# A transformer block on one core: the second MLP product computed with seven block products in place of eight

## The reference

```
h  = rms_norm(x);  proj = h @ w_in                    # 512 tokens, D = 2048
x  = x + merged(attention branches, gates) @ w_out
h2 = rms_norm(x)
u  = relu(h2 @ w_mlp_up)                              # 2048 -> 8192
x  = x + (u * u) @ w_mlp_down                         # 8192 -> 2048
```

## Time and profile before

| | |
|---|---|
| median of 3 runs | 2702.49 us (2702.45 to 2702.6) |
| the profiled execution | 2704.16 us, span 2702.4 us |
| PE, PEld, DVE, ACT, POOL busy | 2693.1, 2396.2, 1712.9, 1179.5, 41.1 us |
| granted PE clock | 1.0 throughout |
| moved from and to HBM | 348.23 MB read, 37.75 MB written |

### The profile page before, as it was taken

One profiled execution on the slowest core, in us unless ns is written; L12 is line 12 of the kernel. 1 busy time (PEld: TensorE's weight loads), 2 busy tenths in 40 slices (PEclk: granted clock), 3 DMA queues, 4 the chain that ended last, 5 costly groups with the idle time before them and its releaser, 6 DMA issues.

```text
span 2702.4 us, 44449 instructions
## 1 busy us (share of the span) xinstructions
PE 2693.1 (100%) x15962; PEld 2396.2 (89%) x15962; DVE 1712.9 (63%) x2978; ACT 1179.5 (44%) x1628; POOL 41.1 (2%) x60
## 2 busy tenths in 40 slices
PE   9999999999999999999999999999999999999999
PEld 8999999788888888888899999999998888888887
DVE  4648887677777754434588788788764444444444
ACT  5534443545555552224354444444443333433343
POOL 0000000000000000000000000000000000000000
PEclk9999999999999999999999999999999999999999
DMA  6444344332232235534343433433456565565653
GB/s 249 119 128 130 125 138 123 96 85 80 72 85 77 79 107 151 142 125 154 119 133 125 135 129 124 140 124 126 138 188 223 187 222 200 193 224 186 226 200 119
DMA packets 359572, 386.96 MB, mean 143 GB/s; under 512 B 16464, under 2 KB 274000, under 8 KB 358992
## 3 DMA queue, kind: packets, MB, share of 16 engines
q1 hardware_dynamic: 331936, 347.24, 40.6%
q10 hardware_dynamic: 27568, 38.81, 4.1%
HBM read 348.23 MB, written 37.75 MB: 143 GB/s over the span
## 4 chain that ended last, share of the span: by engine, by line
PE 98%; DVE 1%; ACT 0%; DMA 0%; issue 0%; SPq 0%; ACTq 0%; DVEq 0%
PE job L1731 7%; PE job L1734 7%; PE job L1733 7%; PE job L2044 2%; PE job L2048 2%; PE job L2046 2%; PE scores L2048 2%; PE scores L2046 2%; PE scores L2044 2%; PE job L2071 2%; PE job L2073 2%; PE job L2072 2%; PE scores L2071 2%; PE scores L2072 2%; PE scores L2073 2%; PE heads_out L1831 1%
## 5 line engine op out<-in xcount | busy, mean ns | idle before, releaser
L1665 DVE TENSOR_TENSOR w_lo_d<-raw_d,w_hi_d 128x512 fp32r<-128x512 f32 x256 | 176.3, 690 | 369.0 <-ACT w_hi_d L1090 369.0
L1393 DVE TENSOR_TENSOR lo<-pair,hi 128x1792 fp32r<-128x1792 f32 x142 | 287.1, 2022 | 122.6 <-ACT hi L862 122.6
L862 ACT ACTIVATE hi<-pair 128x1792 fp32r<-128x1792 f32 x142 | 241.5, 1701 | 276.4 <-PE heads_out L2048 119.6
L1090 ACT ACTIVATE w_hi_d<-raw_d 128x512 fp32r<-128x512 f32 x256 | 161.5, 632 | 405.2 <-PE heads_out L2073 202.8
L697 ACT ACTIVATE w_hi<-raw 128x512 fp32r<-128x512 f32 x268 | 168.8, 631 | 354.7 <-PE job L1734 242.9
L1148 DVE TENSOR_TENSOR w_lo<-raw,w_hi 128x512 fp32r<-128x512 f32 x268 | 186.9, 699 | 157.5 <-ACT w_hi L697 156.4
L1731 PE MATMUL job<-a_hi,w_hi 128*128 128x512 f32 x560 | 229.5, 410 | 0.0
L1734 PE MATMUL job<-a_hi,w_lo 128*128 128x512 f32 x560 | 219.6, 392 | 0.0
L1733 PE MATMUL job<-a_lo,w_hi 128*128 128x512 f32 x560 | 218.6, 390 | 0.0
L2044 PE MATMUL job<-h,hi 128*128 128x256 f32 x512 | 145.1, 283 | 2.2 <-DVE lo L1393 2.1
L1671 DVE TENSOR_TENSOR u_lo<-u_raw,u_hi 128x2048 fp32r<-128x2048 f32 x64 | 146.2, 2284 | 0.0
(11 more groups left out here) (468 smaller groups left out, 7767.1 us busy)
## 6 DMA issues: line engine op xcount, KB each, us to landing
pair<-in_w_mlp_up SPq DMA_DIRECT2D x256, 256.0 KB, 2.9
u_raw<-u_rows SPq DMA_DIRECT2D x64, 1024.0 KB, 5.6
raw_d<-in_w_mlp_down SPq DMA_DIRECT2D x128, 512.0 KB, 6.1
raw<-in_w_in SPq DMA_DIRECT2D x79, 512.0 KB, 4.1
pair<-in_w_gate SPq DMA_DIRECT2D x84, 256.0 KB, 2.9
raw<-in_w_out SPq DMA_DIRECT2D x64, 256.0 KB, 3.3
u_rows<-u_out ACTq DMA_DIRECT2D x32, 512.0 KB, 4.3
raw<-in_w_in SPq DMA_DIRECT2D x24, 344.0 KB, 3.2
```

The costliest lines, as they stand in the source:

```text
L862: nc.scalar.activation(pair_hi[j % 2], pairs[j][:, :, 1:8], ACT.Copy).then_inc(pair_hi_ready, 1)
L1090: nc.scalar.activation(w_hi_d[:, j % SPLITS], raw_d[:, j // 2, j % 2], ACT.Copy).then_inc(down_hi, 1)
L1393: nc.vector.tensor_tensor(pair_lo[j % 2], pairs[j][:, :, 1:8], pair_hi[j % 2].bitcast(F32), ALU.subtract).then_inc(pair_lo_ready, 1)
L1665: nc.vector.tensor_tensor(w_lo_d[:, j % SPLITS], raw_d[:, j // 2, j % 2], w_hi_d[:, j % SPLITS].bitcast(F32), ALU.subtract).then_inc(down_ ...
```

## The change

The second product gets the same seven-for-eight scheme as the first. The weights `w_mlp_down` are the stationary side, in pairs of 128 output columns (`COLS` = 8 pairs of pairs, 256 columns each) and pairs of 128 rows. The 8192 rows of `u*u` are 32 slices. A *group* g takes eight of them, slices g to g+7 modulo 32, times column block g modulo 8; four groups with one column block cover all 32 slices, and there are 32 groups of four units. From one group to the next one slice leaves and one comes in, so 39 slices are loaded in all (`load_slice`, 7 combinations x 256 columns = 896 KB).

- At the end of the first product VectorE forms the combinations of `u*u` (`sum_u`, three operations of 512, 256 and 256 columns) and ScalarE stores 896 KB in place of 512 KB for each pair (`store_u`). In the loop body the store of the even pair stands ahead of the round of unit 0, that of the odd pair behind the round of unit 4.
- `sum_pairs` forms the sums of two units in one go (1024, 512 and 512 columns) at even units, in place of `sum_pair` at each. This holds for the first product too.
- In each group one new slice is rounded (ScalarE, 1792 columns) and split (VectorE, 1792 columns) at unit 3.
- The combined results of groups 0 to 7 are stored by POOL in HBM (`sum_rows`, 512 KB a group); groups 8 to 23 are added to them by accumulating DMAs, each of which waits for the one before. For groups 24 to 31 the sum is loaded, added by VectorE (`total`), turned back to tokens by eight transposes on PE (`turn_out`, ahead of unit 3 of the next group), scaled by ScalarE (`scale_out`, four operations of 256 columns) and added by an accumulating DMA to `out`, in which the residual was stored earlier (no `x2_rows` and no load of it).

```diff
-    x2_rows = nc.dram_tensor("x2_rows", (S, D), F32, kind="Internal").ap()
+    u_rows = nc.dram_tensor("u_rows", (PAIRS, P, 7 * 2 * P), F32, kind="Internal").ap()
+    sum_rows = nc.dram_tensor("sum_rows", (COLS, P, 4 * 2 * P), F32, kind="Internal").ap()
     v_rows = nc.dram_tensor("v_rows", (S, WD + WF), F32, kind="Internal").ap()
...
+            def load_down(g, j):
+
+                sp.wait_ge(pair_lo_ready, down_unit(g, j) - 3)
+                at, cols_of = (g + 2 * j) % PAIRS, slice(2 * P * (g % COLS), 2 * P * (g % COLS + 1))
+                for h in range(2):
+                    into = pairs[j][:, :, 2 * h:2 * h + 2].rearrange("p k i c -> p k (i c)")
+                    if crosses_end(g, j):
+                        sp.dma_start(into[:, 0], wd[h, :, at, cols_of]).then_inc(pair_loaded[j], 16)
+                        sp.dma_start(into[:, 1], wd[h, :, 0, cols_of]).then_inc(pair_loaded[j], 16)
                     else:
+                        sp.dma_start(into, wd[h, :, at:at + 2, cols_of]).then_inc(pair_loaded[j], 16)
+
+            def load_slice(e):
+
+                sp.wait_ge(pair_used, UPS - 3 + e // 2 if e < 8 else down_unit(e - 8, 0) + 1)
+                sp.wait_ge(u_stored, 16 * (e % PAIRS + 1))
+                sp.dma_start(h_slices[e % 8][:, :, 1].bitcast(F32),
+                             u_rows[e % PAIRS].rearrange("p (a s) -> p a s", a=7)).then_inc(slice_loaded[e % 8], 16)
+
+            for g in range(GROUPS):
+                for j in range(4):
+                    load_down(g, j)
+                    if g == 0 and j > 1:
+                        load_slice(2 * j - 4)
+                        load_slice(2 * j - 3)
+                    if g == 1 and j == 0:
+                        for e in range(4, 8):
+                            load_slice(e)
+                    if g > 0 and j == 1 and g + 7 < EVENTS:
+                        load_slice(g + 7)
...
+            def store_part(g):
+
+                pool.wait_ge(c_ready, GATE_PAIRS + PAIRS + g + 1)
+                into = sum_rows[g % COLS].rearrange("p (a s) -> p a s", a=4)
+                if g < COLS:
+                    pool.dma_start(into, blocks[:, 0:4]).then_inc(part_stored, 16)
+                else:
+                    pool.wait_ge(part_stored, 16 * g)
+                    pool.dma_start(into, blocks[:, 0:4], accum_op=ALU.add).then_inc(part_stored, 16)
+
+            def load_sum(g):
...
+            def add_out(g):
+
+                pool.wait_ge(out_scaled, g - CLOSING + 1)
+                q = g % COLS
+                pool.dma_start(outt[:, :, 2 * P * q:2 * P * (q + 1)], out_tok[:, :, :], accum_op=ALU.add
+                               ).then_inc(out_added, 16)
...
+            def store_u(p):
+
+                act.wait_ge(u_summed, p + 1)
+                into = u_rows[p] if isinstance(p, int) else u_rows[bass.ds(p, 1)].rearrange("a p c -> p (a c)")
+                act.dma_start(into, u_blocks[:, 1:8].rearrange("p a s -> p (a s)")).then_inc(u_stored, 16)
...
+                    if m == 0 and not first:
+                        store_u(i * 2 - 2)
...
@@ -1075,62 +1102,62 @@
                     if not (first and m < 4):
                         round_pair(n, m % 4, n - 1)
                     if m == 2 and not first:
-                        finish_pair(i * 2 - 1, 1)
+                        finish_pair(i * 2 - 1)
+                    if m == 4 and not first:
+                        store_u(i * 2 - 1)
                     if m == 6:
-                        finish_pair(i * 2, 0)
+                        finish_pair(i * 2)
 
...
+            def scale_out(g):
+
+                act.wait_ge(out_turned, g - CLOSING + 1)
+                at_least(act, out_added, 16 * (g - CLOSING))
                 for b in range(TB):
+                    last = nc.scalar.activation(out_tok[:, b], bank_sets[g % 2][b // 2][:, 2 * P * (b % 2):2 * P * (b % 2 + 1)],
+                                                ACT.Copy, scale=r2[:, b:b + 1])
+                last.then_inc(out_scaled, 1)
...
+            def sum_pairs(n, j):
...
+                nc.vector.tensor_tensor(t[:, :, 4:6], t[:, :, 1:3], t[:, :, 0:1].broadcast_to([P, 4, 2, P]),
+                                        ALU.add).then_inc(sums_first, 2)
+                dve.wait_ge(sums_first, n + 2)
+                nc.vector.tensor_tensor(t[:, :, 6], t[:, :, 4], t[:, :, 2], ALU.add).then_inc(sums_second, 2)
+                dve.wait_ge(sums_second, n + 2)
+                nc.vector.tensor_tensor(t[:, :, 7], t[:, :, 6], t[:, :, 3], ALU.add).then_inc(sums_ready, 2)
+
...
+            def total(g):
+
+                dve.wait_ge(sum_loaded, 16 * (g - CLOSING + 1))
+                dve.wait_ge(c_fourth, GP + PAIRS + g + 1)
+                dve.wait_ge(c_ready, GP + PAIRS + g + 1)
+                nc.vector.tensor_tensor(sum_in[:, 0:4:2], blocks[:, 0:4:2], sum_in[:, 0:4:2], ALU.add)
+                nc.vector.scalar_tensor_tensor(sum_in[:, 1:4:2], blocks[:, 1:4:2], -1.0, sum_in[:, 1:4:2], ALU.mult,
+                                               ALU.subtract).then_inc(total_ready, 1)
...
+                p = GP + PAIRS + g - 1
+                for j in range(4):
+                    n = down_unit(g, j)
                     if j == 1:
+                        combine_early(p, (g - 1) % 2, blocks)
+                    split_pair(n, j)
+                    if j == 1:
+                        combine_late(p, (g - 1) % 2, blocks)
+                        if g > CLOSING:
+                            total(g - 1)
+                    if g == 0 and j < 3:
+                        split_slice(2 * j + 2)
+                        split_slice(2 * j + 3)
+                    if j % 2 == 0 and n + 2 < down_unit(GROUPS, 0):
+                        sum_pairs(n + 2, (j + 2) % 4)
+                    if j == 3:
+                        if g == 0:
+                            sum_u(PAIRS - 1)
+                        if g + 8 < EVENTS:
+                            split_slice(g + 8)
...
+            def turn_out(g):
+
+                pe.wait_ge(total_ready, g - CLOSING + 1)
+                for b in range(TB):
+                    for i in range(2):
+                        at = 2 * P * (b % 2) + P * i
+                        last = nc.tensor.transpose(bank_sets[g % 2][b // 2][:, at:at + P],
+                                                   sum_in[:, 2 * (b // 2) + 1 - i, P * (b % 2):P * (b % 2 + 1)],
+                                                   ident[:, :])
+                last.then_inc(out_turned, 1)
+
+            for g in range(GROUPS):
+                pe.wait_ge(c_ready, GATE_PAIRS + PAIRS + g - 1)
+                at_least(pe, out_scaled, g - 1 - CLOSING)
+                for j in range(4):
+                    if g > CLOSING and j == 3:
+                        turn_out(g - 1)
+                    pe.wait_ge(slice_ready, g + 2 * j + 2)
+                    up_unit(down_unit(g, j), j, g % 2, at=g)
+            turn_out(GROUPS - 1)
```

More of the change, by code:

```diff
@@ L619, in _ @@
-            sp.wait_ge(pair_used, UPS - 3)
-            for c in range(BLOCKS):
-                down_loads(c, 0)
-                down_loads(c, 1)
-                load_back(c)
-                with sp.Fori(2, KD // (2 * KU)) as turn:
-                    down_loads(c, turn)
+            wd = w_mlp_down[0].rearrange("(s h p) c -> h p s c", h=2, p=P)
+            def load_down(g, j):
[6 more added lines that the diff above has]
+                        sp.dma_start(into[:, 1], wd[h, :, 0, cols_of]).then_inc(pair_loaded[j], 16)
+                    else:
+                        sp.dma_start(into, wd[h, :, at:at + 2, cols_of]).then_inc(pair_loaded[j], 16)
@@ L1120, in _, with round_slice @@
-            round_u(0, 0, 0)
-            for n in range(LEAD):
-                if n == 2:
-                    copy_p1(GP + PAIRS - 1, 1, blocks)
-                round_down(n, n)
-            finish_pair(PAIRS - 1, 1)
-            for c in range(BLOCKS):
-                down_turn(c, 0)
-                with act.Fori(1, KD // (2 * KU) - 1) as turn:
-                    down_turn(c, turn)
-                down_turn(c, KD // (2 * KU) - 1)
-            store_out(BLOCKS - 1)
-            for b in range(TB):
-                act.wait_ge(out_stored[b], 16 * BLOCKS)
+            def round_slice(e):
+                act.wait_ge(slice_loaded[e % 8], 16 * (e // 8 + 1))
+                slot = h_slices[e % 8]
+                nc.scalar.activation(slot[:, :, 0], slot[:, :, 1].bitcast(F32), ACT.Copy).then_inc(slice_hi, 1)
@@ L1136, in _ @@
+            act.wait_ge(total_ready, GROUPS - 1 - CLOSING)
+            copy_p1(GP + PAIRS + GROUPS - 1, (GROUPS - 1) % 2, blocks)
+            scale_out(GROUPS - 1)
         @block.vector
@@ L1621, in _ @@
             split_pair(GU + 1, 1)
[L1622 to L1623 removed]
+            sum_pairs(GU + 2, 2)
             combine_acts(6)
@@ L1647, in up_pairs @@
                         combine_late(i * 2 + GP, 0, blocks)
```

(25 more changed lines are left out.)

301 lines of the change are left out of this document (116 added, 185 removed).

## The result

| | before | after |
|---|---|---|
| median | 2702.55 us (2702.45 to 2702.65) | 2806.99 us (2803.63 to 2811.93) |
| ratio of the runs | | 1.0388, interval 1.037 to 1.0406 |
| span of the profiled run | 2702.4 us | 2801.9 us |

3.9% slower, where 1.3% was forecast. The page after, parts 1, 4 and 5, against the earlier trace rows: PE has gaps now, and the chain, 98% PE before, is 56% PE.

The account below looks back on a forecast made before the run. PE was taken to bound the kernel, the second product by its pace alone. Terms -52.4 + 6.1 + 31 + 10.7 + 17.3 + 7.8 + 10.5 + 5 = +36 gave 2738 us; range 2692 to 2795.

Parts of the forecast that it names:

- Accumulating DMAs elsewhere: Groups 8 to 23 of the second product: adding transfers mostly hidden, sharing DMA engines with slices and weights; +5 us, bounds 0 and 50.
- The prediction's own sign of being wrong: The forecast is wrong if the first product takes 650 us, or the second's groups 20.2 or above 22 us.
- The passage: From unit 0 to unit 1, both products: two units' sums make PE 0.50 us late, 62 times, +31 us.
- The store: First product's loop: even pair's store ahead of unit 0's round makes it 0.71 us late, 15 times, +10.7 us.
- PE's own work: Second product: 128 units of 5.04 us take 645.1 us for 697.5, -52.4 us; transposes add 6.1 us.
- The opening: Start of the second product: eight slices must land, be rounded and split; PE waits, +17.3 us, bounds 8 and 30.
- The tail: After the last matmul: 14 us for 3.5, with 7 us for the accumulating DMA; +10.5 us.
- Passage hidden: Rival at unit 0 to unit 1: two units' sums cost no more than one's; 2685 us, chance 0.17.
- Weights late: Rival in the second product: each group waits for weights at unit 2's sums; 2769 or 2805 us, chance 0.19.
- Slow accumulate: Rival: from 20 us on the accumulating DMA paces groups 8 to 23; 2810 to over 2900 us, chance 0.07.

Follow-up runs that it names:

- single sums: The changed kernel with one unit's block sums at every unit in both products, in place of two units' sums at every second: 2764.88 us, ratio 1.0222.
- the last kernel: The changed kernel with single sums, even-pair store behind the round, slice rounded at unit 1, split at unit 2, opening slices loaded earlier, `scale_out` later: 2687.52 us.

## Why the prediction was wrong

**The failed step is "Accumulating DMAs elsewhere", with what it left out.** It took +5 us for all traffic in the loop, and looked for a consumer of late transfers at the sums of unit 2. The consumer was the slice's round and split at unit 3, in the opening priced with care and in the loop not at all. Moving these two took 31.1 us off groups 8 to 23, loading a seventh of the slice 31.5, plain stores 18.2. So the term was late slices, 31 us, of which 18 went when the transfers beside them didn't add in memory. The prediction's own sign of being wrong, groups above 22 us, came true in groups 8 to 30 (23.05 and 23.15 on average).

**The passage: mechanism right, size too small.** 0.50 forecast; with the store out of the way a group of the first product is 0.68 to 0.74 over: 0.50, 0.14 from the handovers, and up to 0.10 at unit 2. In groups 8 to 23 single sums saved 15.8 us, where 16 x 0.50 = 8 was forecast. They also ended VectorE's waits for late weights there (none between 2220 and 2500 us, 30.1 us in the change), since a sum over two units waits for the weights of both. How much of the 15.8 that is was not taken apart.

**The store: right, 0.71 forecast, 0.95 measured** (14.2 / 15). From the start of the round of unit 3, `sum_u` ends at +5.29 in a passage of the loop (1515.72 to 1521.01), where +5.27 was forecast. From there to the round lie 0.69 us (0.17 to the issue of the store, 0.52 from the issue to the round), where 0.48 was forecast: these two handovers were taken too short.

**PE's own work: right.** Units are 5.04 us wherever nothing is late, in two kernels through 23 groups. A unit behind eight transposes is 5.86: 0.82, for 0.87 forecast.

**The opening: nearly right, 20.3 for 17.3.** Its five gaps were forecast at 4.4, 7.9, 1.1, 3.4 and 0.5 us and measured 5.7, 8.5, 2.2, 2.4 and 1.6, so that one error partly covers the others. The clock had no place in the estimate. PE issued 53 matmuls in 8 us at a mean granted clock of 0.73 (2058 to 2066), 151 ns each for 120. In the whole opening 59 matmuls were issued at 0.50, each some 0.09 us longer than at full clock: an estimate of at most 5.5 us, since waits behind them hide a part.

**The tail: 17.4 us for 14.** The work ahead of the transfer took 7.6 us (2784.47 to 2792.06), where its terms add to 6.6. From the last scaled piece (2790.49 + 1.57) to the end of the span are 9.8 us, 1.3 of them POOL's issue; 7 had been taken for the transfer, from bounds and without a row:

```profile
2792.36 1.30 POOL L688 DMA_DIRECT2D out<-out_tok  x1 [9.71 <-ACT out_tok L1126]
```

**The rivals.** "Passage hidden" fell: single sums save 42 us. "Weights late" had the time nearly right and the place wrong: its 2805 us for 3 us a group, near the measured 2807, is luck. The waits are there, up to 4.1 us, but with the slices out of the way they cost little. "Slow accumulate" fell in its form, since no part waits 20 us, and was right in spirit: the addition costs what stands beside it.

The sign of the prediction held, and mostly for the reasons given: the passage, the store, the opening and the tail came as forecast or larger. The size failed because each engine's fixed order was checked at one place, the passage from unit 0 to unit 1, and not where the change itself had added new waits.

What stays open: why 128 KB of a slice need 7.7 us to land, and how much of the opening's 14 us (in the last kernel) is bytes or VectorE's pieces. The clock's part there is at most some 3 us, by the same estimate (32 matmuls at 0.50).

## What to carry to other kernels

Price a new transfer by who stands behind its consumer on an in-order engine, not by its bytes: the same slices cost 31 us at unit 3 and nothing at units 1 and 2 of the next group, though they landed later. On an engine that is busy 80%, halving the number of operations by doubling their size can cost: 1.0 us more work in one place of a unit of 5 us makes PE late there, and the time saved elsewhere was idle time. The smaller operations made VectorE busier (90% for 77% between 2300 and 2400 us, with later slices) and the kernel faster. And test faults together as well as apart: the sums and the store were worth 6.4 and 14.2 us alone and 35.2 together.

## What was not expected of the hardware

- An adding transfer of 512 KB from SBUF to HBM lands after 7.7 us where a plain one takes 5.3, beside the same slices and weights, and holds POOL for 0.86 us at its issue, for 0.53. Transfers of 896 KB beside it take 9.8 for 8.5.
- PE's granted clock went to and fro between its two levels, 1.00 and 0.50 (2.4 and 1.2 GHz), in the opening of the second product. It was 1.00 up to the end of the first product and at first while PE stood idle for 5.5 us (2038.5 to 2044.0), 0.50 in the stretch below, 1.00 again from 2049 to 2055 us (PE busy for 2.3 us of them), 0.50 from 2056 to 2062 (busy for 4.5), and 1.00 for good from 2076. The 0.74 and 0.73 above are means over both levels. At 0.50 matmuls of 256 columns start 0.21 us apart, for 0.12.

```profile
2042.00:2048.00 6.00, 3.97 (x18) 4.00 (x19) 3.91 (x2) 2.71 (x2) 0.00 (x0) 0.50 0.78 275
```

- The last kernel's PE stood still for only 2.8 us there (2001.4 to 2004.2). It then issued 12 matmuls at full clock, and from 2006 to 2009 us the clock was 0.50.
- In the sums of two units one operation starts 0.10 us after the recorded end of the one it reads, in one unit's sums 0.04; an independent operation starts 0.08 before that end (1399.30 + 0.69 to 1399.91).
